# Two trunk layers written out in each engine's program instead of a loop over layers

## The reference

```python
for l in range(DEPTH):                       # DEPTH = 2
    h = rms_norm(x, norm_mix[l])
    u = h @ w_in[l]                          # one input projection for four head groups
    y_a = mla_mixer(...)                     # latent attention, causal, rotary
    y_b = pool_mixer(...)                    # windowed means
    y_c = swa_mixer(...)                     # attention over a window of 128
    y_d = conv_mixer(...)                    # short gated convolution
    y = rms_norm(stack(y_a, y_b, y_c, y_d), mix_out_norm[l])
    x = x + y @ w_mix_out[l]
    h = rms_norm(x, norm_xa[l])
    m = rms_norm(mem, norm_mem[l])
    x = x + cross_attention(h, m, ...)       # 256 memory tokens
    h = rms_norm(x, norm_ffn[l])
    x = x + hier_moe(h, ...)                 # 32 experts, 2 of 8 in the best of 4 groups
```

## Time and profile before

| | us |
|---|---|
| three runs | 1207.82, 1208.82, 1213.61 |
| median | 1208.82 |
| the profiled execution, time | 1213.07 |
| its span | 1211.4 |
| mean granted TensorE clock | 0.961 |

### The profile page before, as it was taken

How to read it: one execution, slowest core, us unless ns; L and a number is a source line. 1 busy time by engine, 2 the same in 40 slices (tenths; PEclk the granted TensorE clock), 3 DMA queues, 4 the chain that set the end, 5 groups by cost and what they waited for, 6 DMA issues and landing times.

```text
span 1211.4 us, 17891 instructions
## 1 busy us (share of the span) xinstructions
PE 1139.7 (94%) x4956; PEld 622.0 (51%) x4956; DVE 693.7 (57%) x1637; ACT 367.5 (30%) x799; POOL 45.5 (4%) x87
## 2 busy tenths in 40 slices
PE   6999899999789999999889999999996899999996
PEld 3854556556564444444357545555565644444442
DVE  4345574467676555555642375644676755555556
ACT  4215231023433333333142162211143333333330
POOL 8000000000006000000000000000000000000000
PEclk9999898999889999999989998989997999999999
DMA  9140023410319999999440300244004199999991
GB/s 293 39 138 2 1 69 104 190 55 1 136 74 312 422 422 421 422 421 423 183 149 16 124 1 1 70 139 198 11 2 178 38 391 406 422 422 422 421 416 72
DMA packets 53463, 243.16 MB, mean 201 GB/s; under 512 B 8976, under 2 KB 19504, under 8 KB 28048
## 3 DMA queue, kind: packets, MB, share of 16 engines
q1 hardware_dynamic: 49760, 240.40, 50.1%
q0 software_dynamic: 2528, 1.89, 0.8%
q10 hardware_dynamic: 1104, 0.02, 0.0%
HBM read 240.19 MB, written 2.10 MB: 200 GB/s over the span
## 4 chain that ended last, share of the span: by engine, by line
PE 79%; DVE 11%; issue 3%; DVEq 2%; ACT 2%; DMA 1%; ACTq 1%; SPq 0%
PE ps L2634 17%; PE ps L2200 11%; PE ps L2656 9%; PE ps L2444 8%; PE ps L2192 7%; PE ps L2599 5%; PE ps L2170 4%; PE ps L2600 4%; PE ps L2492 2%; PE ps L2224 2%; PE ps L2280 2%; DMA X<-in_x 1%; PE ps L2311 1%; PE ps L2288 1%; DVEq L1288 1%
## 5 line engine op out<-in xcount | busy, mean ns | idle before, releaser
L2634 PE MATMUL ps<-wgu,xw 128*64 128x512 f32 x1024 | 225.4, 592 | 0.5 <-issue 0.5
L2035 DVE TENSOR_TENSOR X<-ps,X 128x512 f32<-128x512 f32 x256 | 156.5, 681 | 14.0 <-issue 13.2
L2200 PE MATMUL ps<-hT,ring 128*128 128x512 f32 x352 | 159.7, 610 | 0.0
L2634 PEld LDWEIGHTS ps<-wgu,xw 128*64 128x64 f32 x1024 | 74.3, 137 | 144.0 <-issue 143.9
L2656 PE MATMUL ps<-wdn,hhT 128*64 128x512 f32 x512 | 119.9, 611 | 2.7 <-ACTq L1233 2.7
L2444 PE MATMUL ps<-ring,yT 128*128 128x512 f32 x256 | 119.2, 615 | 0.4 <-DVE X L1402 0.4
L856 ACT ACTIVATE xw<-xgT 128x512 f32 (+1 forms) x132 | 81.8, 624 | 104.8 <-issue 92.0
L2599 PE MATMUL ps<-yhi,Wt 128*128 128x512 f32 x256 | 107.6, 420 | 4.6 <-DVEq L1288 3.7
L2200 PEld LDWEIGHTS ps<-hT,ring 128*128 128x128 f32 x352 | 67.8, 197 | 79.0 <-issue 79.0
L2600 PE MATMUL ps<-ylo,Wt 128*128 128x512 f32 x256 | 101.1, 395 | 0.0
L2058 DVE SCALAR_TENSOR_TENSOR ylo<-ps,ws,yhi 128x512 fp32r<-128x512 f32 x64 | 48.1, 751 | 63.2 <-ACTq L1250 62.8
(11 more groups left out here) (374 smaller groups left out, 1377.6 us busy)
## 6 DMA issues: line engine op xcount, KB each, us to landing
wgu<-in_w_gate SPq DMA_DIRECT2D x64, 1024.0 KB, 10.5
wgu<-in_w_up SPq DMA_DIRECT2D x64, 1024.0 KB, 12.7
wdn<-in_w_down SPq DMA_DIRECT2D x64, 1024.0 KB, 13.0
ring<-in_w_in SPq DMA_DIRECT2D x8, 1024.0 KB, 6.5
ring<-in_w_mix_out SPq DMA_DIRECT2D x12, 512.0 KB, 5.9
w_kv<-in_xa_w_kv SPq DMA_DIRECT2D x4, 1024.0 KB, 8.2
ring<-in_w_in SPq DMA_DIRECT2D x2, 2048.0 KB, 16.2
ring<-in_w_in SPq DMA_DIRECT2D x2, 1536.0 KB, 16.2
```

The lines of the kernel that those rows point to most:

```text
L2035: tt(xh, bank, xh, ALU.add).then_inc(mfreed((what, n)), 1)
L2200: last = mm(bank, w[:, c, c0:c0 + P], hT[:, c, :], start=c == 0, stop=c == KD - 1)
L2634: last = mm(bank[r], xw[:, c, j, 0:SLOTS], wgu[2 * parity + j][:, :, c, :], start=c == 0, stop=c == KD - 1)
```

## The change

On each of the five engines the loop over layers becomes a Python loop, so that the layer's instructions stand twice, one behind the other, with `l` as 0 and as 1. The values of the waits in the dense part are constants then. The conditions on `l` (the loads of X on SP, the gains on ACT) are decided when the program is built. The last line accounts for the plan's being gone through twice. The inner loops over pairs of experts and their registers stay.

```diff
-            with sp.Fori(0, DEPTH) as l:
+            for l in range(DEPTH):
...
-                with sp.If(l < 1):
+                if l < 1:
                     for t in range(NT):
                         sp.dma_start(X[:, t], x_d[:, t]).then_inc(x_in[t], 16)
...
-            with pool.Fori(0, DEPTH) as l:
+            for l in range(DEPTH):
...
-            with act.Fori(0, DEPTH) as l:
-
-                with act.If(l > 0):
+            for l in range(DEPTH):
+
+                if l > 0:
                     load_gains(l)
...
-            with dve.Fori(0, DEPTH) as l:
+            for l in range(DEPTH):
...
-            with pe.Fori(0, DEPTH) as l:
+            for l in range(DEPTH):
...
-            assert opened == dense.order, "the plan's order is the program's"
+            assert opened == DEPTH * dense.order, "the plan's order is the program's"
```

## The result

The changed kernel takes 1200.17 us (median of 6 runs, 1197.58 to 1202.41), the kernel before 1209.32 (6 runs, 1207.74 to 1213.61): a ratio of 0.9924, 95% interval 0.9907 to 0.9942, so 9.1 us or 0.76% faster. Run once more beside some of the experiments (6 runs) it took 1198.21 against 1208.76, ratio 0.9909 (0.9882 to 0.9937).

A forecast was written before the change was run, and what follows sets the result against it. PE, busy for 94% of the span, was taken as the bound. Seam -4.1, register pieces -2.6, head -0.2 and table loads 0 give -6.9 us, from 1208.82 to 1201.9 us; range 1196 to 1210.

The forecast's parts named there:

- Seam, -4.1: Between layers: without PE's branch back and its fetch, L2311 starts earlier, clock effect included; 4.1 us saved, ends 1.0 to 5.8.
- DVE is free at 607.20: At the seam: from then DVE could do its two products with the gain, ending at 608.8, with L2311 about 608.9.
- Register pieces, -2.6: Layer-dependent register and semaphore pieces in the chain: three quarters of 3.4 us saved, ends 0.5 and 3.9.
- the chain moving to PE cuts the value: Register term's low end: the chain mostly moves to PE, taken to have no register work, leaving 0.5 us.
- the clock at the seam alone: At the seam: one half-clock stretch still counted, costing 1.7 us where L2311 lost 1.2, so 4.7 became 4.2 us.
- Table loads, 0: ACT's load moves from each layer's head to before the first Exp, done before DVE's maximum: 0, worst end 2.6 us.
- Rival 1: At the first Exp, table loads land on the chain and cost 2.6 us: 1204.5 us; chance 0.17.
- Head, -0.2: Kernel's start: SP issues X without four register pieces ahead of it; 0.2 of 0.35 us saved.
- Rival 2: At the seam, the pause is only partly the fetch: 1.0 us saved for 4.1, 1205.0 us; chance 0.15.
- Rival 3: PE's inner pair loop no longer fits and refetches each turn: 17 us lost in one layer, 1219 us; chance 0.06.
- Rival 4: Register work was all hidden and the seam short by chance: about -2, 1207 us; chance 0.06.

The follow-up runs named there:

- e12: Changed kernel with the layer's number loaded into a register on PE alone: 1203.14 us, ratio 0.9952 against the kernel before.
- e1: Kernel before with only PE's layers one behind the other, as two one-turn loops: 1203.70 us, ratio 0.9964.
- e6: Changed kernel with the layer's number loaded into registers on PE, DVE and ACT: 1209.97 us, ratio 1.0014 against the kernel before.
- e4: Kernel before with the change on every engine but PE, which keeps its layer loop: 1204.39 us, ratio 0.9977.
- e2: Kernel before plus a prefetch hint on PE, at the layer's top, for the branch at its end: 1205.88 us, ratio 0.9987.
- e10: Kernel before plus that kind of branch prefetch hint on PE, DVE and ACT: 1210.52 us, ratio 1.0008.
- e5: The changed kernel itself, run again as yardstick: 1198.21 us, ratio 0.9909 against the kernel before.

## Why the prediction was right, and where it was off

The forecast was 1201.9 us; 1200.2 came. The causes were the right ones, the branch back and the register work. That the sum came so near is in part luck: it had no term for the clock outside the seam and priced the register work too low, while the head gave nothing and a part of the seam's gain was register work.

- **Seam, -4.1: right in sum** (-4.2 in the profile), through other terms. One step of it misread a row: 606.59 is the end of the seventh addition. The chain lays the eighth under "DVEq L1288, 0.61", and all eight end at 607.19 (603.10 after: 597.54 and 5.56). So PE had 2.6 us to gain and not 3.3. L2311 starts 613.43 - 607.19 = 6.24 us behind the additions before and 3.55 after: 2.7 us nearer, not 4.7. The half-clock stretch falls on the transposes, 3.55 us for 1.95. DVE's first two products with the gain are over at 605.9, but L2311 stands behind the 16 transposes on PE and starts at 606.65, and not 0.2 us behind DVE. The stretch spares L2311 in return (1.15 us to the first L2192), and the additions themselves begin 0.4 us sooner behind the combining products.
- **What the seam's step left out:** it took all of PE's gain for the fetch. The branch ended at 604.30 + 4.69 = 608.99, 1.8 us behind the additions; the other 0.8 us, to the transpose at 609.97, went with the values of the eight banks, computed in registers (e12 has 0.6 us of it without any branch). And "DVE is free at 607.20" was not so. DVE had a fetch of about 3 us of its own behind that drain (e1). Neither cost the forecast anything, since the change takes the register work away and straightens DVE as well; a forecast for PE alone, made in the same way, would have said 4 us at the seam, where 0.8 came.
- **Register pieces, -2.6: the term that was mis-sized.** The pieces of L585, L591, L603 and L1356 went from the chain: it held 22 of DVE's L585 and L591 and 14 of ACT's L585 before, and 8 and 3 after, 0.02 us each. What they were worth is more: putting them back costs 4.1 us on DVE, 3.9 on PE, nothing measurable on ACT, and on all three 6.7 (5.6 against both sets), their share of the clock included. Whether the two overlap or add up can't be told at 2 us of scatter. Two steps failed: that the chain moving to PE cuts the value (PE had register work too, which the chain doesn't name), and that only the pieces' own time counts.
- **Clock: the term that was missing.** Half-clock time fell from 80 to 68 us. At 0.34 us each that is 4 us of the 9. At equal half-clock time the two kernels differ by 5.0 us (1205.0 for 1200.0, standard errors 0.2 and 0.4). Shorter handoffs leave PE shorter pauses, and I had priced the clock at the seam alone. That the shorter pauses cause this is argued from the table: every kernel with constants on PE and DVE has 65 to 68 us (70 in the changed kernel's first set alone), every one without has 70 to 96.
- **Table loads, 0: right, by the mechanism given**, the load beside the maximum, but with nothing to spare: it was to be over 0.6 us before Exp, and it ends at 98.40, where the maximum ends at 98.37. Rival 1 was as near as I said: e6 shows it at its full 1.28 us a layer.
- **Head, -0.2: not seen.** The first L2192 came at 32.95 us for 32.20; over all the profiles without loads at the head it lies between 32.20 and 33.73, changed or not.
- **Rival 2** (the pause only partly a fetch) falls as it was priced, at 1.0 us for the seam, but it has a grain of truth: of the 2.6 us behind the additions 1.8 are the fetch. **Rival 3** (an inner loop that no longer fits) falls too: a pair in the loop takes 14.57 to 14.63 us in both kernels and both layers, and in the changed kernel the instruction queues move three packets in 190 us of it, where a fetch a turn would need six of PE's alone (380 to 570 us: packets, MB, share).

```profile
q8 instruction: 1, 0.02, 0.0%
q14 instruction: 2, 0.02, 0.0%
```

- **Rival 4** (register work hidden) is the wrong way round: it is worth more than I forecast, and not less.

## What to carry to other kernels

When one engine stands still behind a branch, ask which others branch there too: their pauses lie side by side, the views of waits and of the chain name only the latest, and removing one shows the next. The record of each engine's branch instruction gives its pause by itself. Where DVE hands on to PE all the time, a register instruction ahead of each wait is paid in full and, it seems, again in the clock, so constants in waits were worth more here than their count times 0.08 us; on an engine with slack, here ACT, they are worth nothing, and straightening it only lengthens its program. Before trusting an experiment that should keep register work, see in the trace that it did.

## What the runs showed of the hardware that I had not expected

- The pause at a branch back over a whole layer: DVE's 2.92 us (e1), PE's 4.7 and 4.6 us (before, e4), for 0.08 where PE's branch isn't taken. With a hint executed a whole layer earlier PE's was 2.9 and 3.4 us (e2, e10), and DVE's went to 0.6 (e10). PE's 5.4 us of idle time overlap with 2.9 us that it waits for DVE's additions in the changed kernel too.
- A table load (1.28 us) ahead of an instruction with several waits stood beside the last of them where all were constants, and behind it where they took registers, so the same load is free in one kernel and 1.28 us a layer in the other (e5, e6).
- One register instruction of nine additions takes 0.20 us on DVE and 0.16 on ACT, for 0.04 of a single addition.
- Executions of one kernel differ by up to 13 us (1201.7 to 1214.9 for the kernel before), and their half-clock time goes along with it. A change of 0.5% is near the edge of what a median of six can tell.
